# Decay rows in a buffer of their own, log decays made one head ahead, decayed queries in level two of a hybrid encoder layer

## The chip, the cores and the metric

The kernel runs on one core of a Trainium2 chip. The metric is the device time of one execution in microseconds. A core has five engines with instruction streams of their own: TensorE (PE, matrix products), VectorE (DVE), ScalarE (ACT), GpSimd (POOL) and SyncE (SP, which here only starts DMAs). They wait for each other through semaphores. The products read SBUF and write PSUM banks.

## The reference

One encoder layer over two sequences of 512 tokens, width 1024. One input projection feeds two groups of heads: neighbourhood attention (8 heads) and gated DeltaNet (4 heads of 128, both directions). The part that matters here, per DeltaNet head:

```
qkv = silu(dwconv_centred(concat(g_q, g_k, g_v)))      # 5 taps
q, k = l2norm(q) * dk**-0.5, l2norm(k)
gc = cumsum(g)                                         # log decays, per chunk
decay = exp(where(tril, gc_i - gc_j, -inf))
lower = where(strict, (k beta) k^T * decay, 0);  a = lower + I
solve a [u, w] = [v beta, k beta exp(gc)]
attn = q k^T * decay;  q_dec = q * exp(gc)
scan over chunks: v_new = u - w S;  o = q_dec S + attn v_new;  S = S cd + k_dec^T v_new
o = rmsnorm(o_forward + o_backward) * norm_w * silu(z)
```

The heads' outputs are concatenated with the attention's, projected, normalised, and followed by a gated MLP with a depthwise convolution of width 3 and a second norm.

## The kernel before, in words

The input is held transposed, split into a high and a low part; each projection is made of 24 products per sequence (8 slices of the width, 3 products each: high-high, low-high, high-low). Weights come in chunks of 512 KB: SP loads them into two raw buffers (L417), POOL splits each into high and low parts (L524, L527), and PE uses them in order. SP's loads wait for the split of an earlier chunk, POOL's splits for PE to have finished an older one, so all three follow one counter. Every engine's order of work is written out by hand, and an engine that waits holds up whatever is written behind the wait.

The program first does the attention pairs (`attend`, four pairs, with projections as filler on PE), then the four DeltaNet heads (`delta_head`, h = 0 to 3), the output projection, and the MLP.

One head, in the order in which its work depends on itself:

1. PE projects queries for sequence 0, multiplies keys by keys, and transposes the keys (L803, L808). ACT squares the transposed keys (`key_squares`, L1261); DVE makes the key scales from them (`key_scales`, L1643).
2. Two decay rows per head, broadcast to 128 partitions, come from DRAM into the buffer `egr` (`load_decays`, L465), which shares its place with `d_n`. DVE makes the log decays from them (`log_decays`, L1656) and ACT takes their exponential in place (L1296); the result `dt_` shares its place with `att`. ACT also takes the exponential of `egr` itself (L1301).
3. DVE convolves the queries of sequence 0, then makes the lower blocks (`lower`, L1668), joins and masks them (L1742, semaphore `masked`).
4. PE projects values for sequence 0 into bank 0 once the query convolution has read it, then folds the masked blocks (L820, semaphore `folded`), then projects values for sequence 1 and the gate. ACT centres the value projection (`centre`, L1245) and copies the folded blocks (L1306); SP stores them to DRAM and loads them back turned (L476 to L482).
5. DVE inverts the small blocks (`eliminate`, L1685 to L1700) and the inverses go through DRAM too. DVE expands them: first what PE needs for level 0 (x_1 and m_t, L1705), then, behind the decayed queries (`decayed_q`, L1679), what DVE itself updates (d_n, L1705).
6. Three levels (lv = 0, 1, 2) double the block size: PE makes two groups of products per sequence (L872, then L886 and L889), ACT copies between them, DVE updates and selects (L1785, L1786, L1724, L1728). PE puts pieces of the next head's key projection in between as filler; the last head has none.
7. A scan over four chunks (k = 0 to 3), then the sums for the norm (L942, L943). SP waits for those sums before it loads the next head's decay rows, since `d_n` is in use until then. The next head's keys are convolved, the norm is finished and the tile goes to `mix`.

`mix` has eight tiles: four from the attention pairs, four from the heads; all are read by the output projection (`high_mix` on ACT, `low_mix` on DVE).

Of the kernel before, what the change touches and what calls it, by code (L numbers as in the profile page):

```python
# [11 lines left out]
P = 128  # L12
# [35 lines left out]
FILL = 2  # L48
LN_EPS, RMS_EPS = 1e-5, 1e-6
# [36 lines left out]
def encoder_layer(nc, xT, x_tok, ln_row, w_gate, w_all, rpb, gdn_conv, gate_vec, a_log,  # L86
                  norm_w, ffn_conv, consts, nat_mask, y, block_dram, inverse_dram, x1_dram, decay_dram):
    from contextlib import ExitStack
    ctx = ExitStack()
    with ctx:  # L90
# [131 lines left out]
        dt_, egr = att, d_n  # L222
# [101 lines left out]
        mix_high, mix_ready = sem("mix_high"), sem("mix_ready")  # L324

# [55 lines left out]
        def unit(n):  # L381
            return n // BLOCKS, n % BLOCKS

# [28 lines left out]
        def _(sp):  # L412
# [54 lines left out]
            load_chunks(8, GDN0 + 4)  # L467
            sp.wait_ge(o_evac, 2 * PAIRS + 1)
            load_decays(0)
            load_chunks(GDN0 + 4, GDN0 + 6)  # L470

            def exchange(h, last_head):
# [27 lines left out]
                for n in range(8, 10):  # L500
                    load(raw(GDN0 + n), 4 * h + (GDN0 + n))
# [3 lines left out]
            load_chunks(GDN0 + 4 * GH + 6, CHUNKS)  # L505
# [11 lines left out]
        def _(pool):  # L517
# [29 lines left out]
            split_chunks(2, GDN0 + 4)  # L547
# [6 lines left out]
            def split_for_next(h, last_head):  # L554

                pool.wait_ge(inv_ready, h + 1)
# [4 lines left out]
                if not last_head:  # L561
                    split_later(h, 2)
                    split_later(h, 3)
# [38 lines left out]
        def _(pe):  # L602
# [189 lines left out]
            def delta_head(h, last_head):  # L792
# [21 lines left out]
                project(0, slot(GDN0 + 2), 0)  # L814
                pe.wait_ge(k_tok_ready, 2 * h + 1)
                for s in range(SEQS):
                    pe.wait_ge(masked, 2 * h + (s + 1))
                    for cc in range(CH):
                        n = s * CH + cc
                        ins = mm(ps[6][:, n * IB:(n + 1) * IB], tile(u_t[:, s, :], cc), fold, start=True, stop=True)  # L820
                ins.then_inc(folded, 1)
# [74 lines left out]
                for k in range(CH):  # L896
# [20 lines left out]
                    for g in range(GROUPS):  # L917
# [13 lines left out]
                        ins = mm(out, x_1[:, g, P:2 * P], tile(att[:, g, :], cc), start=k == 0 and g % 2 == 0,  # L931
# [189 lines left out]
        def _(act_e):  # L1121
# [84 lines left out]

            def attend(pair, last_pair):
# [6 lines left out]
                for n in range(1, UNITS + 2):  # L1214
                    if n >= 2:
                        turned(pair, n - 2)
                    if 2 <= n < UNITS:
                        exps(pair, n)
                    if not last_pair and n in done_at:
# [31 lines left out]
            def delta_head(h, last_head):  # L1251
# [64 lines left out]
                for lv in range(NL):  # L1316
                    for s in range(SEQS):
                        act_e.wait_ge(x1_done, 2 * NL * h + (2 * lv + s + 1))
                        nc.scalar.copy(x_1[:, s, :], ps[2 + s][:, :]).then_inc(x1_evac, 1)

                for k in range(CH):
# [9 lines left out]
                    if k < SEQS:  # L1331
                        if k == 0:

                            act_e.wait_ge(ud_ready, 4 * h + 4)
                            if last_head:
                                high_mix(0)
# [11 lines left out]
                nc.scalar.preload_act_table_set(LN_EXP)  # L1348
# [144 lines left out]
        def _(dve):  # L1493
# [90 lines left out]
            def attend(pair, last_pair):  # L1584
# [3 lines left out]
                for n in range(2, UNITS):  # L1588
                    biased(pair, n)
                    normalised(pair, n - 1)  # L1590
                    if n == 7:
# [13 lines left out]
            attend(PAIRS - 2, False)  # L1605
            attend(PAIRS - 1, True)


            def tile(ap, c):
                return ap[:, c * P:(c + 1) * P]  # L1610
# [28 lines left out]
            def delta_head(h, last_head):  # L1639
# [10 lines left out]
                def log_decays(g):  # L1650

                    s, d = g // 2, g % 2
                    dve.wait_ge(rows_landed, 32 * h + 32)
                    for cc in range(CH):
                        col = NEG_GC * 16 + d * 8 + s * CH + cc
# [420 lines left out]
```

## Time and profile before

| what | value |
|---|---|
| median of 3 runs | 1462.19 us (1462.02 to 1463.68) |
| the profiled execution | 1462.43 us, span 1460.6 us |
| granted PE clock, mean | 0.989 of full |
| busy: PE, DVE, ACT, POOL | 96%, 54%, 30%, 33% |
| granted PE clock, 241 to 636 us (the heads) | 0.96 |
| decay rows, SP issue to landing, 8 transfers of 512 KB | 4.8 us (median) |
| mean of a split's two halves, L524 and L527 | 1.895 and 2.539 us |
| POOL's wait for PE before the split at 176.35 us | 13.84 us |
| longest idle of DVE ahead of an update of the scan, L1820 | 2.1 us |
| idle of DVE ahead of the key convolution of head 2 | 2.59 us |
| idle of ACT ahead of the scan of head 1 | 3.74 us |
| a table load on ACT | 1.28 us |

The span is that of the instructions; the device time of the same execution is 1.8 us longer. A bracket at the end of a row gives how long the engine was idle ahead of it and who ended that. Rows of the chain are pieces that ended last, followed back from the end, so their times add up. Rows of a timeline may merge several instructions (x8), and successive instructions of DVE and ACT overlap by about a tenth of a microsecond.

### The profile page before, as it was taken

To read this page: it belongs to the slowest core of one execution; us is meant where nothing else is said; L and a number is where in the kernel's file an instruction comes from. 1 tells how busy PE (TensorE), PEld (TensorE's weight loads), DVE (VectorE), ACT (ScalarE), POOL (GpSimd) and SP (SyncE) were. 2 spreads that over 40 slices of the span, in tenths; PEclk is the share of its full clock that TensorE was granted. 3 is DMA by queue.
4 is the path that set the end of the run, shared out by engine and by line. 5 is a ranking of instruction groups with operands and counts; after the bars stand their busy time and mean duration, and the time that the engine had idled before them with its cause. 6 is when DMAs were issued, how large, how long until landed. Compare 5 with 4: busy or idle time off the path is not lost.

```text
span 1460.6 us, 18720 instructions
## 1 busy us (share of the span) xinstructions
PE 1397.9 (96%) x6959; PEld 1147.7 (79%) x6959; DVE 789.3 (54%) x1346; ACT 441.7 (30%) x924; POOL 479.7 (33%) x219
## 2 busy tenths in 40 slices
PE   7999998989899898799999999999999999999998
PEld 5777776778787787788878888888888888888886
DVE  4344446877958869742654344344344344225657
ACT  4233344427236164240532212211221222122220
POOL 3322221212121122116454334334334344454470
PEclk9999999999999999899999999999999999999999
DMA  8100111201102112032221111111111114111112
GB/s 248 45 30 30 34 40 44 50 9 59 41 15 64 29 59 49 15 130 86 102 87 44 56 45 43 57 43 43 57 43 43 57 43 187 57 43 46 55 57 101
DMA packets 49511, 87.15 MB, mean 60 GB/s; under 512 B 24432, under 2 KB 27184, under 8 KB 49456
## 3 DMA queue, kind: packets, MB, share of 16 engines
q1 hardware_dynamic: 44704, 70.41, 15.4%
q10 hardware_dynamic: 4752, 15.99, 2.8%
q8 instruction: 36, 0.59, 0.2%
q14 instruction: 19, 0.16, 0.0%
HBM read 76.66 MB, written 9.73 MB: 59 GB/s over the span
## 4 chain that ended last, share of the span: by engine, by line
issue 37%; PE 33%; DVE 15%; POOL 10%; DMA 2%; ACT 1%; POOLq 1%; SPq 0%; DVEq 0%; ACTq 0%
PE banks L639 11%; POOL w_hi L524 8%; PE banks L955 6%; PE banks L1055 3%; PE banks L614 2%; DVE qkv L1623 2%; PE banks L748 1%; DMA d_n<-decay_dram 1%; PE banks L773 1%; DVE m_t L1668 1%; DVE d_n L1786 1%; PE banks L761 1%; DVE inv L1697 1%; DVE outer L1694 1%; DVE att L1656 1%
## 5 line engine op out<-in xcount | busy, mean ns | idle before, releaser
L524 POOL TENSOR_TENSOR w_hi<-w_raw,one 128x1024 fp32r<-128x1024 f32 (+1 forms) x99 | 187.6, 1895 | 905.7 <-PE banks L614 376.0
L614 PE MATMUL banks<-x_hi,w_hi 128*128 128x512 f32 (+1 forms) x912 | 360.3, 395 | 19.1 <-POOL w_lo L527 8.9
L614 PE MATMUL banks<-x_hi,w_lo 128*128 128x512 f32 (+1 forms) x912 | 356.9, 391 | 0.0
L614 PE MATMUL banks<-x_lo,w_hi 128*128 128x512 f32 (+1 forms) x912 | 356.6, 391 | 0.0
L1907 DVE SCALAR_TENSOR_TENSOR cv<-banks,fw,cv 128x511 f32<-128x511 f32 x176 | 131.9, 750 | 261.7 <-ACT cv L1427 254.0
L527 POOL TENSOR_TENSOR w_lo<-w_raw,w_hi 128x1024 fp32r<-128x1024 f32 (+1 forms) x99 | 251.3, 2539 | 7.8
L614 PEld LDWEIGHTS banks<-x_hi,w_hi 128*128 128x128 f32 (+1 forms) x912 | 171.3, 188 | 58.5 <-issue 11.4
L614 PEld LDWEIGHTS banks<-x_hi,w_lo 128*128 128x128 f32 (+1 forms) x912 | 171.1, 188 | 37.5 <-issue 1.0
L614 PEld LDWEIGHTS banks<-x_lo,w_hi 128*128 128x128 f32 (+1 forms) x912 | 171.4, 188 | 36.9 <-issue 1.5
L1427 ACT ACTIVATE cv<-banks,fw_j 128x512 f32<-128x512 f32 x88 | 68.7, 780 | 336.9 <-PE banks L614 334.4
L1936 DVE TENSOR_TENSOR a_lo<-act,a_hi 128x1024 fp32r<-128x1024 f32 x39 | 65.5, 1684 | 96.1 <-ACT a_hi L1445 96.1
L1055 PE MATMUL banks<-w_hi,a_hi 128*128 128x512 f32 x288 | 112.0, 389 | 0.0
L1055 PE MATMUL banks<-w_hi,a_lo 128*128 128x512 f32 x288 | 112.0, 389 | 0.0
L1055 PE MATMUL banks<-w_lo,a_hi 128*128 128x512 f32 x288 | 112.0, 389 | 0.0
L639 PE MATMUL banks<-x_hi,w_hi 128*128 128x512 f32 x256 | 103.9, 406 | 0.0
L639 PE MATMUL banks<-x_lo,w_hi 128*128 128x512 f32 x256 | 103.3, 404 | 0.0
L639 PE MATMUL banks<-x_hi,w_lo 128*128 128x512 f32 x256 | 103.3, 404 | 0.0
L1445 ACT CAST a_hi<-act 128x1024 fp32r<-128x1024 f32 (+1 forms) x39 | 40.8, 1054 | 147.3 <-PE banks L1055 139.7
L1623 DVE SCALAR_TENSOR_TENSOR qkv<-banks,cw_all,qkv 128x510 f32<-128x510 f32 (+1 forms) x96 | 71.2, 749 | 12.1 <-ACT qkv L1245 8.8
L1917 DVE TENSOR_TENSOR act<-cv 128x512 f32 (+1 forms) x44 | 68.4, 1554 | 9.1 <-DVE cv L1907 8.9
L1564 DVE TENSOR_TENSOR s_sb<-banks,bm 128x512 f32<-128x512 f32 x32 | 22.1, 691 | 76.8 <-PE banks L748 76.8
L1055 PEld LDWEIGHTS banks<-w_lo,a_hi 128*128 128x128 f32 x288 | 54.1, 188 | 11.3
(206 smaller groups left out, 1999.9 us busy)
## 6 DMA issues: line engine op xcount, KB each, us to landing
w_raw<-w_all SPq DMA_DIRECT2D x102, 512.0 KB, 3.3
d_n<-decay_dram SPq DMA_DIRECT2D x8, 512.0 KB, 4.8
z_tok<-x_tok ACTq DMA_DIRECT2D x8, 512.0 KB, 5.6
x_dram<-z_tok ACTq DMA_DIRECT2D x8, 512.0 KB, 2.6
z<-x_dram ACTq DMA_DIRECT2D x8, 512.0 KB, 7.5
y<-z SPq DMA_DIRECT2D x7, 512.0 KB, 2.6
mix<-xT SPq DMA_DIRECT2D x12, 256.0 KB, 7.7
gb<-ln_row ACTq DMA_DIRECT2D x4, 512.0 KB, 7.9
```

The lines of the kernel that those rows point to most:

```text
L524: nc.gpsimd.tensor_tensor(w_hi[u][:, 0:n], w_raw[ru][:, 0:n], one[:, :].to_broadcast([P, n]), ALU.mult).then_inc(w_high, 1)
L527: nc.gpsimd.tensor_tensor(w_lo[u][:, 0:n], w_raw[ru][:, 0:n], w_hi[u][:, 0:n].bitcast(F32), ALU.subtract).then_inc(w_ready, 1)
L614: last = mm(ps[bank][0:cols, :], w[u][:, k * cols:(k + 1) * cols], seq(x[:, k, :], s), start=n == 0, stop=n == 3 * KT - 1)
L639: ins = mm(ps[s][:, :], w[u][:, k * P:(k + 1) * P], seq(x[:, k, :], s), start=i == 0, stop=i == 3 * KT - 1)
L955: ins = mm(ps[b][:, :], x[k][:, t * P:(t + 1) * P], w[u][:, cols], start=k == 0 and n == 0, stop=k == KT - 1 and n == 2)
L1055: ins = mm(ps[t][:, :], x[a][:, t * P:(t + 1) * P], w[u][:, cols], start=start and i == 0, stop=stop and i == 2)
L1427: A(cv[:, b, :], ps[b][:, :], ACT.Identity, scale=fw_j[:, x, 1:2], bias=fw_j[:, x, 3:4]).then_inc(up_center, 1)
L1445: nc.scalar.copy(a_hi[a][:, :], act[:, bass.ds(k, 1), :].rearrange("p a n -> p (a n)")).then_inc(a_high, 1)
L1623: ins = STT(dst[:, a:b], src[:, a + o:b + o], cw_all[:, 3 * h + x, tap:tap + 1], dst[:, a:b], ALU.mult, ALU.add)
L1907: ins = STT(cv[:, b, a:e], ps[b][:, a + o:e + o], fw[:, bass.ds(2 * j + x, 1), tap:tap + 1].rearrange("p a b -> p (a b)"), cv[:, b, a:e], ...
L1917: TT(act[:, bass.ds(j, 1), s * L:(s + 1) * L].rearrange("p a n -> p (a n)"), cv[:, s, :], cv[:, 2 + s, :], ALU.mult).then_inc(up_act, 1)
L1936: TT(a_lo[a][:, :], act[:, bass.ds(k, 1), :].rearrange("p a n -> p (a n)"), a_hi[a][:, :].bitcast(F32), ALU.subtract).then_inc(a_ready, 1)
```

## The change

- The decay rows get a place of their own, the first two tiles of `mix`. Their attention output is stored to DRAM (`mix_dram`) once two pairs are done, and ACT loads it back in the last head. `egr` therefore no longer shares with `d_n`.
- The log decays of head h have a buffer that alternates (`dt_(h)`: two further tiles of `mix`, or `att`). Those of head 0 are made during the attention; of a later head three of four groups are made in the scan of the head before, the fourth at the head's start. The rows of the next head are loaded once the decayed queries of this one are made.
- The decayed queries are made in the loop of levels at lv == 1, no longer between the expansions.
- The fold of the masked blocks stands inside the value projection, ahead of the slice FOLD_AT = 5 of 8.
- Weights: one chunk fewer is split ahead of the heads; a head's gate chunk is split once its blocks are masked. ACT centres the queries of sequence 1 ahead of the exponentials of `egr`, and loads its table ahead of the scan instead of behind it.

```diff
@@ places @@
+FOLD_AT = 5
-        dt_, egr = att, d_n
+        egr = mix[:, 0:2, :].rearrange("p k (s n) -> p (k s) n", s=SEQS)
+        decays = [mix[:, 6:8, :].rearrange("p k (s n) -> p (k s) n", s=SEQS), att[:, :, :]]
+        def dt_(h):
+            return decays[h % 2]
@@ SyncE @@
-            load_chunks(8, GDN0 + 4)
-            sp.wait_ge(o_evac, 2 * PAIRS + 1)
+            load_chunks(8, 12)
+            sp.wait_ge(o_evac, 2 * 2 + 1)
+            sp.dma_start(mix_dram, flat(mix[:, 0:2, :])).then_inc(mix_stored, 16)
+            sp.wait_ge(mix_stored, 16)
             load_decays(0)
-            load_chunks(GDN0 + 4, GDN0 + 6)
+            load_chunks(12, GDN0 + 5)
...
-                for n in range(6, 8):
+                for n in range(5, 7):
                     load(raw(GDN0 + n), 4 * h + (GDN0 + n))
                 if not last_head:
-
-                    sp.wait_ge(osum_done, 2 * h + 2)
+                    sp.wait_ge(qd_ready, 4 * h + 4)
                     load_decays(h + 1)
@@ GpSimd @@
-            split_chunks(2, GDN0 + 4)
+            split_chunks(2, GDN0 + 3)
...
+                pool.wait_ge(masked, 2 * h + 2)
+                split_later(h, -1)
                 pool.wait_ge(inv_ready, h + 1)
                 split_later(h, 0)
...
                 if not last_head:
                     split_later(h, 2)
-                    split_later(h, 3)
@@ TensorE @@
-                project(0, slot(GDN0 + 2), 0)
-                pe.wait_ge(k_tok_ready, 2 * h + 1)
-                for s in range(SEQS):
-                    pe.wait_ge(masked, 2 * h + (s + 1))
...
+                def fold_blocks(k):
+                    if k != FOLD_AT:
+                        return
+                    pe.wait_ge(k_tok_ready, 2 * h + 1)
+                    for s in range(SEQS):
+                        pe.wait_ge(masked, 2 * h + (s + 1))
+                        for cc in range(CH):
+                            n = s * CH + cc
+                            ins = mm(ps[6][:, n * IB:(n + 1) * IB], tile(u_t[:, s, :], cc), fold, start=True, stop=True)
+                    ins.then_inc(folded, 1)
+
+                project(0, slot(GDN0 + 2), 0, wait_k=fold_blocks)
@@ ScalarE @@
+            def decayed(h, g):
+                act_e.wait_ge(dt_ready, 4 * h + (g + 1))
+                A(dt_(h)[:, g, :], dt_(h)[:, g, :], ACT.Exp).then_inc(dt_exp, 1)
...
-                for g in range(GROUPS):
-                    act_e.wait_ge(dt_ready, 4 * h + (g + 1))
-                    A(dt_[:, g, :], dt_[:, g, :], ACT.Exp).then_inc(dt_exp, 1)
+                if h:
+                    decayed(h, GROUPS - 1)
...
                 key_norms()
+                centre(h, QX, 1)
                 for g in range(GROUPS):
                     A(egr[:, g, :], egr[:, g, :], ACT.Exp).then_inc(egr_ready, 1)
-                centre(h, QX, 1)
                 silu(QX, 0)
                 centre(h, VX, 0)
                 act_e.wait_ge(folded, h + 1)
...
+                    if last_head and lv == 1:
+                        act_e.wait_ge(qd_ready, 4 * h + 4)
+                        act_e.wait_ge(mix_stored, 16)
+                        act_e.dma_start(flat(mix[:, 0:2, :]), mix_dram).then_inc(mix_landed, 16)
+                nc.scalar.preload_act_table_set(LN_EXP)
...
+                    if not last_head and k == 2:
+                        decayed(h + 1, 0)
...
-                nc.scalar.preload_act_table_set(LN_EXP)
+                else:
+                    decayed(h + 1, 1)
+                    decayed(h + 1, 2)
@@ VectorE @@
-                for g in range(GROUPS):
-                    log_decays(g)
+                if h:
+                    log_decays(h, GROUPS - 1)
                 key_scales()
...
-                dve.wait_ge(silu_done, 6 * h + 4)
-                for g in range(GROUPS):
-                    decayed_q(g)
-
-                dve.wait_ge(qd_ready, 4 * h + 4)
...
+                    if lv == 1:
+                        dve.wait_ge(silu_done, 6 * h + 4)
+                        for g in range(GROUPS):
+                            decayed_q(g)
...
+                    if not last_head and k == 1:
+                        log_decays(h + 1, 0)
+                    if not last_head and k == 3:
+                        log_decays(h + 1, 1)
+                        log_decays(h + 1, 2)
```

ACT at the start of head 1, from the key squares to the copy of the folded blocks (`packed`); `att`, `d_n` and `mix` hold the decays, `qkv` the projections that are centred. Before:

```order
L1296 ACTIVATE att<-att 128x512 [waits dt_ready] x4
L1298 COPY k_tok<-banks 128x512 x2
L1268 ACTIVATE k_ln<-k_sq,eps 128x8 [waits k_squared]
L1270 ACTIVATE k_norm<-k_ln 128x8 [waits norm_ln]
L1301 ACTIVATE d_n<-d_n 128x512 x4
L1245 ACTIVATE qkv<-banks,cw_all 128x512 [waits proj_done]
L1254 ACT_TABLE_LOAD
L1254 ACTIVATE qkv<-qkv 128x512 [waits conv_done]
L1245 ACTIVATE qkv<-banks,cw_all 128x512 [waits proj_done]
L1306 COPY packed<-banks 128x128 [waits folded]
```

With the change:

```order
L1223 ACTIVATE att<-att 128x512 [waits dt_ready]
L1317 COPY k_tok<-banks 128x512 x2
L1288 ACTIVATE k_ln<-k_sq,eps 128x8 [waits k_squared]
L1290 ACTIVATE k_norm<-k_ln 128x8 [waits norm_ln]
L1265 ACTIVATE qkv<-banks,cw_all 128x512 [waits proj_done]
L1321 ACTIVATE mix<-mix 128x512 x4
L1274 ACT_TABLE_LOAD
L1274 ACTIVATE qkv<-qkv 128x512 [waits conv_done]
L1265 ACTIVATE qkv<-banks,cw_all 128x512 [waits proj_done]
L1325 COPY packed<-banks 128x128 [waits folded]
```

Three of the four exponentials of the decays are gone from here (they stand in the head before), and the centring behind `key_norms` (L1245, now L1265) comes ahead of the exponentials of the rows. In both, the centring that waits for the value projection stands ahead of the copy that waits for the fold.

PE around the fold of head 1 (`cst,u_t` are the fold matrix and the masked blocks; `x_hi,w_hi` and the like a projection). Before:

```order
L614 MATMUL banks<-x_hi,w_lo_69 128x512
L820 MATMUL banks<-cst,u_t 128x16 [waits masked,k_tok_ready]
L820 MATMUL banks<-cst,u_t 128x16 x3
L820 MATMUL banks<-cst,u_t 128x16 [waits masked]
L820 MATMUL banks<-cst,u_t 128x16 x3
L614 MATMUL banks<-x_hi,w_hi_68 128x512 [waits m_ready]
L614 MATMUL banks<-x_lo,w_hi_68 128x512
```

With the change:

```order
L622 MATMUL banks<-x_hi,w_lo_69 128x512
L831 MATMUL banks<-cst,u_t 128x16 [waits masked,k_tok_ready]
L831 MATMUL banks<-cst,u_t 128x16 x3
L831 MATMUL banks<-cst,u_t 128x16 [waits masked]
L831 MATMUL banks<-cst,u_t 128x16 x3
L622 MATMUL banks<-x_hi,w_hi_68 128x512
L622 MATMUL banks<-x_lo,w_hi_68 128x512
```

The fold comes nine products earlier in the order: before, the product behind it is the first of the next value projection (it waits for `m_ready`); now it is the 16th of the same one.

DVE in head 1, from the expansions to level 1 (`q_d` are the decayed queries, `d_n` the blocks that DVE updates). Before:

```order
L1705 TENSOR_TENSOR m_t<-packed,cst 128x512 x2
L1679 TENSOR_TENSOR q_d<-qkv,d_n 128x512 [waits egr_ready,silu_done]
L1679 TENSOR_TENSOR q_d<-qkv,d_n 128x512 [waits egr_ready] x3
L1705 TENSOR_TENSOR d_n<-packed,cst 128x512 [waits qd_ready]
L1705 TENSOR_TENSOR d_n<-packed,cst 128x512 x3
L1720 TENSOR_TENSOR u_t<-m_t,cst 128x512 [waits expanded]
L1720 TENSOR_TENSOR u_t<-m_t,cst 128x512
L1785 TENSOR_TENSOR d_n<-d_n,banks 128x512 [waits yy_done]
L1786 TENSOR_TENSOR d_n<-d_n,banks 128x512
L1724 TENSOR_TENSOR x_145<-d_n,cst 128x512 [waits w_updated]
```

With the change, at the place where they stood:

```order
L1736 TENSOR_TENSOR m_t<-packed,cst 128x512 x2
L1736 TENSOR_TENSOR d_n<-packed,cst 128x512 x4
L1751 TENSOR_TENSOR u_t<-m_t,cst 128x512 [waits expanded]
L1751 TENSOR_TENSOR u_t<-m_t,cst 128x512
L1815 TENSOR_TENSOR d_n<-d_n,banks 128x512 [waits yy_done]
L1816 TENSOR_TENSOR d_n<-d_n,banks 128x512
```

And at the place where they stand now, two updates later on DVE:

```order
L1755 TENSOR_TENSOR x_145<-d_n,cst 128x512 [waits w_updated]
L1759 TENSOR_TENSOR m_t<-d_n,cst 128x512 [waits v_updated]
L1751 TENSOR_TENSOR u_t<-m_t,cst 128x512 [waits x1_done] x2
L1710 TENSOR_TENSOR q_d<-qkv,mix 128x512 [waits egr_ready,silu_done]
L1710 TENSOR_TENSOR q_d<-qkv,mix 128x512 [waits egr_ready] x3
L1815 TENSOR_TENSOR d_n<-d_n,banks 128x512 [waits yy_done]
```

The four products of the decayed queries leave the place between `m_t` and `d_n`; behind `d_n` DVE goes straight to the first update, and makes the queries behind the blocks of the next level.

## Rows read from the trace of the kernel before

**Rows 1.** Chain that ended last, head 1: start us, us, what

```profile
350.95 4.29 DVE att L1656 x16
...
365.02 0.70 DVE u_t L1742
...
365.76 1.08 PE banks L820 x8
...
367.16 2.14 DMA block_dram<-packed
...
369.81 2.25 DMA blk<-block_dram
...
372.20 0.40 DVE blk L1685
```

**Rows 2.** DVE timeline, key scales of heads 0, 1, 2: start, us, engine, line, operation

```profile
258.03 0.17 DVE L1643 TENSOR_SCALAR k_inv<-k_sq 128x8 f32<-128x8 f32 x1 [5.16 <-ACT x L1261]
...
355.16 0.16 DVE L1643 TENSOR_SCALAR k_inv<-k_sq 128x8 f32<-128x8 f32 x1
...
451.71 0.16 DVE L1643 TENSOR_SCALAR k_inv<-k_sq 128x8 f32<-128x8 f32 x1
```

**Rows 3.** ACT timeline, first square of the keys in heads 0, 1, 2

```profile
255.82 0.28 ACT L1261 ACTIVATE x<-banks 128x128 f32<-128x128 f32 x1 [0.29 <-PE banks L808]
...
352.60 0.28 ACT L1261 ACTIVATE x<-banks 128x128 f32<-128x128 f32 x1 [0.29 <-PE banks L808]
...
448.25 0.28 ACT L1261 ACTIVATE x<-banks 128x128 f32<-128x128 f32 x1 [0.29 <-PE banks L808]
```

**Rows 4.** PE timeline, head 1, first value projection and the next one

```profile
359.07 0.47 PE L614 MATMUL banks<-x_hi,w_hi 128*128 128x512 f32 x1 [0.67 <-DVE qkv L1623]
...
362.59 0.39 PE L614 MATMUL banks<-x_hi,w_hi 128*128 128x512 f32 x1
...
366.68 0.49 PE L614 MATMUL banks<-x_hi,w_hi 128*128 128x512 f32 x1
...
368.62 0.40 PE L614 MATMUL banks<-x_hi,w_lo 128*128 128x512 f32 x1
```

**Rows 5.** ACT timeline, head 1, centring and the copy of folded blocks

```profile
364.83 0.69 ACT L1245 ACTIVATE qkv<-banks,cw_all 128x512 f32<-128x512 f32 x1 [1.98 <-PE banks L614]
366.87 0.27 ACT L1306 COPY packed<-banks 128x128 f32<-128x128 f32 x1 [1.34 <-PE banks L820]
```

**Rows 6.** DVE timeline, head 1, levels 0 and 1

```profile
391.38 2.49 DVE L1679 TENSOR_TENSOR q_d<-qkv,d_n 128x512 f32<-128x512 f32 x4
...
397.65 0.68 DVE L1785 TENSOR_TENSOR d_n<-d_n,banks 128x512 f32<-128x512 f32 x1
...
402.45 1.29 DVE L1720 TENSOR_TENSOR u_t<-m_t,cst 128x512 f32<-128x512 f32 x2
406.19 0.69 DVE L1785 TENSOR_TENSOR d_n<-d_n,banks 128x512 f32<-128x512 f32 x1 [2.45 <-PE banks L889]
```

**Rows 7.** PE timeline, level 0 of heads 0 and 1

```profile
292.74 2.02 PE L872 MATMUL banks<-x,u_t 128*128 128x128 f32 x16 [2.35 <-issue]
...
389.76 3.59 PE L872 MATMUL banks<-x,u_t 128*128 128x128 f32 x16 [2.34 <-issue]
...
395.29 1.06 PE L889 MATMUL banks<-m_t,x 128*128 128x128 f32 x8
```

**Rows 8.** Stretches: from:to, us, then busy us of each engine, granted PE clock

```profile
245.80:249.80 4.00, 4.00 (x10) 3.13 (x11) 3.89 (x9) 1.15 (x2) 0.00 (x0) 0.50 0.46 176
358.00:366.70 8.70, 7.86 (x43) 6.36 (x41) 8.56 (x24) 5.48 (x10) 4.30 (x2) 1.00 0.19 60
389.70:393.10 3.40, 3.34 (x17) 3.37 (x17) 3.40 (x6) 0.58 (x1) 0.00 (x0) 0.54 0.00 0
```

**Rows 9.** Chain that ended last, second group of level 1, heads 0 and 1

```profile
305.06 2.05 PE banks L872 x8
...
402.08 1.13 PE banks L872 x8
```

More of the change, by code:

```diff
@@ L324, in encoder_layer @@
         mix_high, mix_ready = sem("mix_high"), sem("mix_ready")
+        mix_stored, mix_landed = sem("mix_stored"), sem("mix_landed")
         out_step, out_done, out_evac, gb_landed = (
@@ L493, in exchange @@
                                      rows[:, i0:i0 + INST // 2, :]).then_inc(landed, 16)
-                for n in range(6, 8):
+                for n in range(5, 7):
                     load(raw(GDN0 + n), 4 * h + (GDN0 + n))
                 if not last_head:
-                    sp.wait_ge(osum_done, 2 * h + 2)
+                    sp.wait_ge(qd_ready, 4 * h + 4)
                     load_decays(h + 1)
-                for n in range(8, 10):
+                for n in range(7, 9):
                     load(raw(GDN0 + n), 4 * h + (GDN0 + n))
@@ L504, in _ @@
                 exchange(h, h == GH - 1)
-            load_chunks(GDN0 + 4 * GH + 6, CHUNKS)
+            load_chunks(GDN0 + 4 * GH + 5, CHUNKS)
             for t in range(TILES):
@@ L813, in delta_head @@
                 pe.wait_ge(conv_done, 6 * h + 3)
-                project(0, slot(GDN0 + 2), 0)
-                pe.wait_ge(k_tok_ready, 2 * h + 1)
-                for s in range(SEQS):
-                    pe.wait_ge(masked, 2 * h + (s + 1))
[L818 to L821, printed above, removed]
+                def fold_blocks(k):
[9 more added lines that the diff above has]
+                project(0, slot(GDN0 + 2), 0, wait_k=fold_blocks)
                 pe.wait_ge(m_ready, 4 * h + 4)
@@ L928, in delta_head @@
                             pe.wait_ge(qd_ready, 4 * h + 4)
-                        ins = mm(out, x_1[:, g, P:2 * P], tile(att[:, g, :], cc), start=k == 0 and g % 2 == 0,
+                        ins = mm(out, x_1[:, g, P:2 * P], tile(dt_(h)[:, g, :], cc), start=k == 0 and g % 2 == 0,
                                  stop=k == CH - 1 and g % 2 == 1)
@@ L1218, in attend @@
                         exps(pair, n)
+                    if last_pair and 2 <= n < 2 + GROUPS:
+                        decayed(0, n - 2)
                     if not last_pair and n in done_at:
@@ L1335, in delta_head @@
                             if last_head:
+                                act_e.wait_ge(mix_landed, 16)
                                 high_mix(0)
@@ L1582, in attended, with tile, log_decays, attend @@
                     ps[6 + s][:, :].rearrange("p (b r c) -> p r b c", b=BLOCKS, r=ROWS)).then_inc(o_evac, 1)
-            def attend(pair, last_pair):
+            def tile(ap, c):
+                return ap[:, c * P:(c + 1) * P]
+            def log_decays(h, g):
+                s, d = g // 2, g % 2
+                dve.wait_ge(rows_landed, 32 * h + 32)
+                for cc in range(CH):
+                    col = NEG_GC * 16 + d * 8 + s * CH + cc
+                    ins = STT(tile(dt_(h)[:, g, :], cc), tile(egr[:, g, :], cc), sc[:, h, col:col + 1], negm[d],
+                              ALU.add, ALU.add)
+                ins.then_inc(dt_ready, 1)
+            def attend(pair, last_pair, decays_from=UNITS):
                 biased(pair, 0)
@@ L1590, in attend @@
                     normalised(pair, n - 1)
+                    if n >= decays_from:
+                        log_decays(0, n - decays_from)
                     if n == 7:
@@ L1604, in _ @@
             step.leave(PAIRS // 2 - 1)
[L1605 removed]
+            attend(PAIRS - 2, False, UNITS - GROUPS)
             attend(PAIRS - 1, True)
[L1609 to L1610 removed]
             dve.wait_ge(par_landed, 48)
@@ L1648, in key_scales @@
                     dve.wait_ge(scales_ready, h + 1)
[L1650 to L1655, printed above, removed]
-                        ins = STT(tile(dt_[:, g, :], cc), tile(egr[:, g, :], cc), sc[:, h, col:col + 1], negm[d],
-                                  ALU.add, ALU.add)
-                    ins.then_inc(dt_ready, 1)
                 def lower(g):
@@ L1996, in build @@
     decay_dram = nc.dram_tensor("decay_dram", (2, GH, T), F32, kind="Internal").ap()
+    mix_dram = nc.dram_tensor("mix_dram", (P, 2 * T), F32, kind="Internal").ap()
     encoder_layer(nc, y=y, block_dram=block_dram, inverse_dram=inverse_dram, x1_dram=x1_dram, decay_dram=decay_dram,
-                  **args)
+                  mix_dram=mix_dram, **args)
 def shape_constants():
```

6 lines of the change are left out of this document (3 added, 3 removed).

## The prediction, made before the changed kernel was run

> **What bounds the kernel now.** I read the busy shares, then the chain of waits over the four DeltaNet heads (241 to 634 us), then the timelines of TensorE (PE), VectorE (DVE) and ScalarE (ACT) around the places that the change touches. PE is busy nearly all the time, and outside the heads its products follow each other almost without a gap; there only transfers and splits could hurt. Inside a head the chain is a round trip between engines, so what counts is who comes last.
>
> In head 1 that chain runs so [rows 1]: 16 log-decay steps on DVE end at 355.24, then key scales, query convolution, the lower blocks and two masks, the last of which ends at 365.72; PE folds the blocks, ACT copies them, two DMAs turn them (store from 367.16, load from 369.81), and DVE starts the elimination at 372.20. From there DVE is last as far as the levels, where PE and DVE alternate. Head 1 stands for heads 1 to 3; head 0 enters differently.
>
> **Log decays in the head before.** They leave the path, but the next instruction, the key scales, also needs ACT's squares of the keys. Head 0 shows it: its decays are made early, and DVE then sits idle 5.16 us until the squares are done [rows 2]. There the key scales start 2.21 us after ACT's first square (258.03 less 255.82) [rows 2, 3]. Squares need the transposed keys, which PE makes behind the query projection; nothing of that moves. So in head 1 the key scales could start at 352.60 + 2.21 = 354.81 instead of 355.16: 0.35 us gained, not 4.29. In head 2, where the rows' transfer was slower, 448.25 + 2.21 = 450.46 against 451.71: 1.25 us. Head 3 is as head 1. Sum: -1.95 us. Below this it could give 0, if the one group of decays that is left at the head's start were late; it has some 4 us of idle DVE for four steps of 0.27 us (4.29 / 16).
>
> The moved decays cost nothing where they land. Four steps (1.07 us) stand in the scan where DVE idles up to 2.1 us, eight (2.14 us) ahead of the key convolution, where it idles 2.59 us; ACT's table load (1.28 us) moves to where ACT idles 3.74 us; its two exponentials (about 0.56 us each) take the load's old place. If such a cover failed, the excess would be paid once a head, some tenths.
>
> **The fold inside the value projection.** Here something is lost. Before, the 24 products of the first value projection are done when the last mask comes. Now the wait for both masks stands ahead of the 16th product. In head 1 the 16th started at 362.59, 3.52 us after the first [rows 4], and the masks end at about 365.4 (365.72 less 0.35): PE stops about 3 us with nine products in hand. The fold comes no earlier, since DVE sets it. But the projection ends later, and on ACT the centring of that very projection stands ahead of the copy of the folded blocks. Nine products behind the fold last from 366.68 to 368.62 + 0.40 = 2.34 us [rows 4]; ACT takes them up 0.04 us later and its centring holds the copy back by another 0.6 of its 0.69 us [rows 5]. The copy then starts at 366.68 + 2.34 + 0.04 + 0.60 = 369.66 instead of 366.87: 2.8 us later, and with it store, load and elimination. Before, DVE had 0.1 us left there (372.06, when the load lands, against 372.20) [rows 1], so 2.7 us a head, in all four heads: +10.8 us. From below: even with the copy in time, the value convolution (about 3.1 us) and two short fills would end near 373.2 and cost 1.0 us a head (+4.0).
>
> From above: in that stop PE does little for about 4 us (wait, fold, wait, fold), and its clock can fall. The row of 358.00 to 366.70, with a shorter such stretch, still shows 1.00; that of 245.80, behind PE's long wait at the start of head 0, 0.50, with 10 products in 4.00 us [rows 8]. At that pace nine products take 9 x (0.40 - 0.24) = 1.5 us more. Between 0 and 1.5 us a head I take half: +3.0 us.
> The Trainium skill (TensorE: Matmul & The Clock Gate, Part 1) says that the clock depends on how busy the array has lately been, and that being throttled is its idle state, so it speaks against adding a stop. By it the upper end would hold in each head, +6.0 instead of +3.0. The trace agrees only in part: after 2.34 us of waiting the products ran at half pace, after 2.35 us at full pace [rows 7].
>
> **Decayed queries in level one.** (The change's loop calls it lv == 1, the second of three levels.) The four products of 2.49 us leave the place between two expansions, where they were on the path [rows 6], so DVE reaches the first update of level 0 2.45 us earlier. Then PE may be late: its products of level 0 for the first sequence end at 395.29 + 1.06 = 396.35, 6.6 us after it began at 389.76, while DVE took them up at 397.65 [rows 6, 7]. Only 1.3 us were spare, so 1.3 us are gained where PE's first 16 products take 3.59 us, and all 2.45 where they take 2.02, as in head 0 [rows 7]. The slow case is the half clock (0.54 over that stretch) [rows 8]. I take 1.9 us for heads 0 to 2 and 2.4 us for head 3, which has no filler products: -8.1 us; bounds -5.2 and -9.8.
>
> In the new place DVE waited 2.45 us for PE [rows 6], just as long as the products take: no more than 0.1 us is paid, unless that level runs faster than in head 1. A second gain: in three heads (0, 2, 3) level 1 ran at half clock, since PE stood idle between the levels; its second group took 2.05 us in head 0 against 1.13 in head 1 [rows 9]. With DVE earlier that idle time shrinks to what head 1 has: 0.9 x 3 = -2.7 us; bounds 0 and -2.7.
>
> **Queues.** SyncE now stores two tiles (1 MB) and waits for that, then loads the decay rows, all ahead of the 12th chunk of weights. GpSimd still waited 13.8 us for PE at the split in question, so several us of delay are covered; were they not, PE would wait for weights once. The split of the gate chunk moves behind the masks; it takes 1.9 + 2.5 us, and 33 products of 0.24 us (7.9 us) lie between the fold and its user. The tiles come back during the last head's levels over ACT's queue, over 10 us before they are read. All at 0.
>
> **Sum.** -1.95 + 10.8 + 3.0 - 8.1 - 2.7 = +1.05 us. The profiled execution has 1462.43 us (span 1460.6 and 1.8 around it), 0.24 above the median of the runs. Forecast: 1462.43 + 1.05 = 1463.5 us, less 0.24: about 1463.3. A measurement of this kernel can tell about 0.2% (2.9 us) from no change; the forecast lies inside.
>
> **Rivals.**
> - Faster: the clock holds in the stop, and level 0 runs at full pace. -1.95 + 10.8 - 9.8 - 2.7 = -3.65: about 1458.6. For it: the row with 1.00 around the old fold. Against it: the stop is twice as long as there. If moreover the copy were not late (only 1.0 a head), -10.4: 1452; the order of ACT speaks against that. Should the decays give all their 4.29 us in three heads, some 11 us more would go; the 5.16 us of head 0 say no. Together 0.31.
> - Slower, one mechanism: the stop in the value projection lowers PE's clock in every head. +10.8 + 6.0 for the late copy, only -5.2 from the queries as level 0 stays at half pace, no gain in level 1, -1.95: +9.65, about 1472. It decides as soon as the nine products take clearly over 3 us in most heads. For it: 0.50 after the longer wait. Against it: 2.35 us passed unpunished [rows 7]. From +2.9 us up: 0.29.
> - The forecast, within 2.9 us of before: 0.40. Two sizeable terms of opposite sign nearly cancel.
>
> So faster 0.31, same 0.40, slower 0.29. The range takes in both clock cases and nearly the whole way to the cheap fold: 1453 to 1472; the forecast's own part is 1459.3 to 1465.1.
>
> **What would show it.** Right, step by step: DVE idle some 4 us ahead of the key scales in all heads; PE waiting for a mask ahead of the fold with nine products behind it; the copy of the blocks starting over 9 x 0.24 us after the fold; DVE waiting for a DMA ahead of the elimination by 1.5 to 3 us; no query products ahead of the expansions, and a first update of level 0 that waits for PE or comes at once. Wrong: an elimination that starts no later after the masks than the 6.5 us of before (372.20 less 365.72), which would make the kernel about 0.7% faster; or PE waiting for weights in the attention part; or log decays that hold up the scan.

## The result and the profile after

| | before | with the change |
|---|---|---|
| median of 5 runs | 1462.19 us (1462.02 to 1464.63) | 1473.77 us (1468.45 to 1475.6) |
| ratio, 95% interval | | 1.0073 (1.0055 to 1.0090) |
| profiled execution, span | 1462.43, 1460.6 us | 1473.57, 1471.8 us |

The changed kernel is slower by 0.73%: the slower rival, which had a chance of 0.29, and 1.8 us above the top of the range. The page of the changed kernel, busy time and the chain by engine:

```profile
PE 1408.7 (96%) x6959; PEld 1156.7 (79%) x6959; DVE 790.2 (54%) x1346; ACT 441.3 (30%) x924; POOL 479.4 (33%) x219
...
PE 39%; issue 37%; POOL 10%; DVE 10%; ACT 2%; DMA 1%; POOLq 1%; SPq 0%; DVEq 0%; ACTq 0%
```

PE has 10.8 us more busy time than before (1397.9) for the same products: they ran slower. The heads tell where. The table cuts each head at six events of the timelines: the start of ACT's first square of the keys, the end of DVE's last mask, the start of the elimination, of the first update and of the scan's first mask on DVE, and the end of PE's last sum over `d_n`. It adds up four heads of the profiled execution (us); e1 and so on are the experiments below.

| stretch | before | after | e1 | e2 | e3 | e4 | e5 | e8 | e11 |
|---|---|---|---|---|---|---|---|---|---|
| first key square to last mask | 53.1 | 51.1 | 51.1 | 51.1 | 51.1 | 51.1 | 51.1 | 39.1 | 39.0 |
| last mask to elimination | 26.4 | 46.0 | 26.7 | 36.4 | 39.8 | 31.9 | 26.8 | 30.6 | 29.2 |
| elimination to first update | 101.8 | 95.5 | 94.0 | 91.6 | 95.0 | 93.0 | 101.2 | 91.7 | 91.6 |
| first update to scan | 70.9 | 67.8 | 68.0 | 66.8 | 68.2 | 68.2 | 67.6 | 68.0 | 66.4 |
| scan to the sums' end | 100.0 | 101.2 | 101.3 | 101.0 | 100.0 | 101.0 | 101.3 | 100.0 | 97.1 |

Before against after, in hundredths: -2.05 + 19.62 - 6.28 - 3.13 + 1.26 = 9.4 us when the output projection starts (9.5 by its own rows), and 1.7 us more behind it: the 11.2 us of the spans. One row carries the loss.

Head 1, the chain (start, us, what), against [rows 1]:

```profile
355.48 2.18 ACT x L1281 x16
...
367.56 0.70 DVE u_t L1773
368.31 1.06 PE banks L831 x8
369.37 14.67 PE banks L622 x57
...
393.58 2.49 issue
396.07 2.53 PE banks L885 x16
```

The log decays have gone from its head. Behind the fold it no longer goes over the copy and the two DMAs: it stays on PE, with the nine products that the fold's wait held up and the 48 of the next two projections. But PE is not the bound as far as level 0: it stands 2.49 us ("issue") ahead of that level, and starts when the first of DVE's expansions (`x<-packed,cst`, below) is done. DVE's late start is in the next rows.

PE of the changed kernel, head 1 (timeline), against [rows 4, 7]:

```profile
364.87 0.39 PE L622 MATMUL banks<-x_hi,w_lo 128*128 128x512 f32 x1
367.07 1.04 PE L831 MATMUL banks<-cst,u_t 128*128 128x16 f32 x8 [1.81 <-DVE u_t L1773]
368.31 1.06 PE L831 MATMUL banks<-cst,u_t 128*128 128x16 f32 x8 [0.20 <-DVE u_t L1773]
369.22 0.47 PE L622 MATMUL banks<-x_hi,w_hi 128*128 128x512 f32 x1
...
370.33 0.63 PE L622 MATMUL banks<-x_lo,w_hi 128*128 128x512 f32 x1
...
372.04 0.63 PE L622 MATMUL banks<-x_hi,w_lo 128*128 128x512 f32 x1
...
396.07 2.53 PE L885 MATMUL banks<-x,u_t 128*128 128x128 f32 x16 [2.49 <-issue]
```

ACT, against [rows 5]:

```profile
372.70 0.69 ACT L1265 ACTIVATE qkv<-banks,cw_all 128x512 f32<-128x512 f32 x1 [6.67 <-PE banks L622]
373.29 0.26 ACT L1325 COPY packed<-banks 128x128 f32<-128x128 f32 x1
```

And DVE, against [rows 2, 6]:

```profile
357.69 0.17 DVE L1684 TENSOR_SCALAR k_inv<-k_sq 128x8 f32<-128x8 f32 x1 [4.16 <-ACT x L1281]
...
378.52 0.39 DVE L1716 COPY blk<-packed 64x256 f32<-64x256 f32 x1 [1.56 <-DMA blk<-block_dram]
...
395.28 1.29 DVE L1736 TENSOR_TENSOR x<-packed,cst 128x512 f32<-128x512 f32 x2
...
402.66 0.69 DVE L1815 TENSOR_TENSOR d_n<-d_n,banks 128x512 f32<-128x512 f32 x1 [1.15 <-PE banks L902]
...
408.67 2.49 DVE L1710 TENSOR_TENSOR q_d<-qkv,mix 128x512 f32<-128x512 f32 x4
```

Read together: PE stops 1.81 us ahead of the fold; of the nine products behind it the fifth to ninth take 0.63 us instead of 0.39; ACT sits idle 6.67 us until they are done, centres, and only then copies the blocks that were folded at 369.37. DVE waits for their DMA. The granted clock from the fold to the copy, heads 0 to 3 (from:to, us, busy PE, PEld, DVE, ACT, POOL, then clock), against [rows 8]:

```profile
267.40:275.30 7.90, 7.84 (x29) 6.91 (x30) 4.12 (x6) 0.51 (x1) 4.26 (x2) 0.57 0.00 0
...
367.00:373.20 6.20, 5.93 (x27) 5.05 (x28) 4.13 (x6) 0.50 (x1) 4.26 (x2) 0.75 0.00 0
464.80:472.60 7.80, 7.62 (x27) 6.54 (x28) 4.13 (x6) 0.54 (x1) 4.26 (x2) 0.56 0.01 2
564.10:571.90 7.80, 7.74 (x28) 6.78 (x29) 4.12 (x6) 0.54 (x1) 4.26 (x2) 0.56 0.01 2
```

In three heads almost the whole stretch, fold included, ran at the lower level (1.2 GHz); in head 1 about half of it.

### The profile page after: what moved, and what is told of

Its sections match the earlier page's. It is cut to its first block, busy times and chain, and to the rows that moved or that the text cites. A ratio compares the mean times of both kernels' runs of the same rounds, so it can differ in the third digit from the quotient of the medians.

```text
span 1471.8 us, 18722 instructions
## 1 busy us (share of the span) xinstructions
PE 1408.7 (96%) x6959; PEld 1156.7 (79%) x6959; DVE 790.2 (54%) x1346; ACT 441.3 (30%) x924; POOL 479.4 (33%) x219
## 4 chain that ended last, share of the span: by engine, by line
PE 39%; issue 37%; POOL 10%; DVE 10%; ACT 2%; DMA 1%; POOLq 1%; SPq 0%; DVEq 0%; ACTq 0%
PE banks L647 12%; POOL w_hi L531 8%; PE banks L622 6%; PE banks L968 5%; PE banks L1068 3%; PE banks L885 1%; PE banks L756 1%; DVE qkv L1664 1%; PE banks L781 1%; DVE m_t L1699 1%; DVE d_n L1816 1%; PE banks L769 1%; PE banks L936 1%; PE banks L944 1%; PE banks L927 1%
## 5 line engine op out<-in xcount | busy, mean ns | idle before, releaser
L622 PE MATMUL banks<-x_hi,w_hi 128*128 128x512 f32 (+1 forms) x912 | 364.0, 399 | 17.5 <-POOL w_lo L534 8.3
L622 PE MATMUL banks<-x_lo,w_hi 128*128 128x512 f32 (+1 forms) x912 | 360.3, 395 | 0.0
L1068 PEld LDWEIGHTS banks<-w_hi,a_hi 128*128 128x128 f32 x288 | 54.1, 188 | 11.3
```

Source lines behind the costliest of these rows:

```text
L622: last = mm(ps[bank][0:cols, :], w[u][:, k * cols:(k + 1) * cols], seq(x[:, k, :], s), start=n == 0, stop=n == 3 * KT - 1)
L1068: ins = mm(ps[t][:, :], x[a][:, t * P:(t + 1) * P], w[u][:, cols], start=start and i == 0, stop=stop and i == 2)
```

## The experiments

Theory A: the stop inside the value projection, with products in hand and ACT's order behind them, makes the whole loss; the other parts gain. Rivals stand with each run. Each ratio is to the kernel before on the same chip; it took 1462.16 us beside e1 to e4, 1463.55 beside e5 to e8 and 1463.88 beside e9 to e11, so times of different groups differ by up to 1.7 us for that alone.

**e1, the fold back behind the projection.**

```diff
-                project(0, slot(GDN0 + 2), 0, wait_k=fold_blocks)
+                project(0, slot(GDN0 + 2), 0)
+                fold_blocks(FOLD_AT)
```

> The changed kernel with the fold back behind the first value projection; all else as changed. Theory A (the stop inside the value projection and the slow products behind it hold back ACT's centring, and with it the copy of the folded blocks; together 19.6 us over four heads, from the last mask to the elimination 10.3, 10.3, 11.8 and 11.8 us instead of 6.5 to 6.9): the stretch from last mask to elimination is 6.5 to 6.9 us again in all heads, time 1451 to 1455 us. Theory B (the elimination is late because of another part: ACT's new order, SyncE's queue, the mask itself): the stretch stays above 9 us, time about 1474 us.

Measured 1452.43 us, ratio 0.9936 (0.9920 to 0.9952). Last mask to elimination 6.50, 6.49, 7.18 and 6.49 us (in the changed kernel it is 12.07, 10.27, 11.78 and 11.83 us; the expectation's 10.3 for head 0 is wrong). ACT's copy follows the fold again, and level 0 starts at full pace here behind as long a wait as before:

```profile
362.98 0.27 ACT L1326 COPY packed<-banks 128x128 f32<-128x128 f32 x1 [1.35 <-PE banks L831]
```

```profile
385.86 2.02 PE L886 MATMUL banks<-x,u_t 128*128 128x128 f32 x16 [2.38 <-issue]
```

So one line of the change turns 0.6% gained into 0.7% lost. Theory B is out.

**e2, ACT's copy ahead of the centring.**

```diff
-                centre(h, VX, 0)
                 act_e.wait_ge(folded, h + 1)
                 nc.scalar.copy(packed..., ps[6]...).then_inc(fold_copied, 1)
+                centre(h, VX, 0)
```

> The changed kernel with ACT's copy of the folded blocks ahead of its centring of the value projection; the fold stays ahead of the sixth slice. Theory A: the copy starts within 0.1 us of the fold's end, but DVE still takes the value convolution ahead of the elimination and that waits for the nine late products: the elimination comes only 1.0 to 1.5 us earlier a head, time 1468 to 1470 us. Rival C (ACT's order alone makes the loss): masks to elimination back to 6.5 us, time about 1454 us.

Measured 1459.94 us, ratio 0.9982 (0.9973 to 0.9991): between the two. The order on ACT is not all (rival C), since now the value convolution ends last, as expected:

```profile
364.41 0.27 ACT L1324 COPY packed<-banks 128x128 f32<-128x128 f32 x1 [3.37 <-PE banks L831]
...
368.87 3.10 DVE L1664 SCALAR_TENSOR_TENSOR qkv<-banks,cw_all,qkv 128x510 f32<-128x510 f32 x4 [2.61 <-ACT qkv L1265]
...
372.44 0.38 DVE L1716 COPY blk<-packed 64x256 f32<-64x256 f32 x1
```

But the size was missed by 8 us: the elimination came 2.4 us earlier a head, the fold ran at full pace in all heads here (2.3 us against 3.1 to 3.4 in three heads of the changed kernel), and level 0 too (elimination to first update 91.6). PE's order was not touched, and it stopped as long ahead of the fold (1.77 to 1.81 us); its clock fell later, so the same stop cost 5.9 us of slow products over four heads here.

**e3, PE kept busy in the stop.**

```diff
                     pe.wait_ge(k_tok_ready, 2 * h + 1)
+                    for j in range(8):
+                        mm(ps[6][:, :], w_hi[slot(GDN0 + 2)][:, 0:P], seq(x_hi[:, 0, :], 0), start=True, stop=True)
                     for s in range(SEQS):
```

> The changed kernel with eight extra full-width products on PE ahead of the fold's wait (about 1.9 us; the fold overwrites what they write). Theory A with the clock as its second half: PE stays at full pace, the nine products behind the fold take 2.2 to 2.4 us instead of 3.3 to 4.1, the copy comes 2.7 us late a head as the prediction's order term has it, time 1464 to 1466 us. Rival D (the clock falls with the narrow products of the fold whatever stands ahead of it, or it was only the order): no faster than the changed kernel, 1473 to 1476 us.

Measured 1467.22 us, ratio 1.0033 (1.0021 to 1.0045), 1.2 us above the expected range. With the extra products the clock held in heads 0 and 2; in 1 and 3 it fell behind the fold:

```profile
267.50:273.00 5.50, 5.24 (x31) 4.55 (x31) 4.35 (x8) 0.84 (x3) 3.99 (x2) 1.00 0.00 0
364.10:371.00 6.90, 6.63 (x31) 5.48 (x30) 4.25 (x7) 0.71 (x2) 4.26 (x2) 0.75 0.00 0
462.30:468.00 5.70, 5.44 (x32) 4.72 (x32) 4.53 (x7) 1.06 (x3) 4.22 (x2) 1.00 0.01 3
558.80:565.70 6.90, 6.64 (x30) 5.58 (x30) 4.21 (x7) 0.68 (x2) 4.26 (x2) 0.75 0.00 0
```

This separates the loss in two. Where the clock held, the copy comes 3.88 and 3.91 us behind the last mask, against 1.16 before: 2.73 us a head is the price of the order. In the changed kernel it comes 6.74, 5.04, 6.60 and 6.60 us behind; the clock is the rest, 24.98 - 4 x 3.89 = 9.4 us. Rival D is out as a whole, but not for heads 1 and 3: PE did not stand still ahead of the fold there and only 0.27 us within it, against 0.2 in the kernel before, and the products behind it still ran slow. That the clock's share comes from the stop alone is not shown.

**e4, FOLD_AT = 7 instead of 5.**

> The changed kernel with the fold ahead of the eighth slice of the value projection instead of the sixth: three products behind it instead of nine. Theory A: the copy is late by 3 x 0.24 to 3 x 0.43 us and 0.6 us of centring, 1.3 to 1.9 us a head, instead of 3.8 to 5.6; time 1458 to 1461 us. Theory B: no change, 1474 us.

Measured 1456.30 us, ratio 0.9967 (0.9955 to 0.9980), 1.7 us below the expected range. The stop is short (0.41 to 0.46 us), and from the fold to the copy the clock holds in heads 0 and 1, and nearly in head 3; here heads 1 and 2:

```profile
363.53 1.04 PE L831 MATMUL banks<-cst,u_t 128*128 128x16 f32 x8 [0.46 <-DVE u_t L1773]
```

```profile
363.50:367.30 3.80, 3.57 (x23) 3.24 (x24) 3.66 (x6) 0.64 (x2) 2.43 (x2) 1.00 0.00 0
457.50:462.00 4.50, 4.21 (x22) 3.67 (x23) 4.14 (x6) 0.71 (x2) 3.08 (x2) 0.76 0.02 4
```

The copy is 1.4 us late in three heads and 1.9 in one. The loss falls with the products behind the fold, as theory A has it; the stop is shorter too, and this run does not part the two.

**e5, on e1: the decayed queries back between the expansions** (`decayed_q` out of the loop of levels, to where it stood; it still reads its own decay buffer).

> The kernel of e1 (fold behind the projection) with the decayed queries back between the two expansions, from their own decay buffer. Theory A (the move takes 2.49 us of DVE out of the path and so brings PE into levels 0 and 1 at a faster clock; elimination to first update 94.0 instead of 101.8 us over four heads, first update to scan 68.0 instead of 70.9): both go back to the sums of before, time 1452.4 + 7.7 + 2.9 = 1463 us. Rival F (only the first of the two comes from the queries, the faster level 1 from something else in the change): 1460 us.

Measured 1460.79 us, ratio 0.9984 (0.9969 to 0.9998), 8.4 us above e1 (7.0 by the two ratios), and the table has the reason: elimination to first update 101.2 instead of 94.0 us, but first update to scan 67.6, as fast as with the move. Rival F holds: the queries earn the first term, and the faster levels do not need them. Second group of level 1 of head 0 in e5:

```profile
306.25 1.13 PE L886 MATMUL banks<-x,u_t 128*128 128x128 f32 x8 [1.27 <-DVE x L1756]
```

In the kernel before the same products took 2.05 us [rows 9], also behind a wait of 1.27 us. The waits of that level are the same with the queries on the path (1.88 and 1.27 us against 2.01 and 1.27); only the pace differs, so the 2.9 us are once more the clock. What kept it up there with the change is not shown.

**e6, on e1: all log decays at the head's start; e10, on e6: their rows loaded late as well.**

```diff
                 if h:
-                    log_decays(h, GROUPS - 1)
+                    for g in range(GROUPS):
+                        log_decays(h, g)
```

(The exponentials on ACT likewise, and their calls in the scan go; e10 also waits for `osum_done` instead of `qd_ready` ahead of `load_decays`.)

> The kernel of e1 with all four groups of log decays and their exponentials at the head's start again (heads 1 to 3), from the separate buffer; their rows are still loaded early. Theory A (the key scales wait for ACT's squares in any case, so the move earns only the 2.0 us by which first square to last mask is shorter): since the rows now lie ready, DVE has its decays done long before the squares, and the time stays within 0.5 us of e1 or rises by up to 2, 1452 to 1454.5 us. Rival G (the move takes 3.2 us off the path in each of three heads): 1462 us.

> The kernel of e6 (all log decays at the head's start) with the next head's decay rows loaded only once the sums of this head are done, as in the kernel before. Theory A (what the log-decay part earns comes from loading the rows early into a place of their own, not from where the decays are made): first square to last mask goes back from 12.77 us to 13.1, 14.0 and 13.1 us in heads 1 to 3, 2.0 us in all. Rival K (place of the decays matters, or the rows come in time anyway): 12.8 us in all heads.

Measured: e6 1452.95 us, ratio 0.9939 (0.9918 to 0.9961), as e1; first square to last mask 12.77 us in each head. e10 1457.94 us in one run; that stretch is 12.93, 15.17 and 13.63 us in heads 1 to 3, so 3.4 us are lost, more than the 2.0 expected. Decays and key scales of head 2 in e6, then key scales of head 2 and decays of head 3 in e10:

```profile
439.20 4.29 DVE L1620 SCALAR_TENSOR_TENSOR mix<-mix,sc,cst 128x128 f32<-128x128 f32 x16
444.50 0.17 DVE L1681 TENSOR_SCALAR k_inv<-k_sq 128x8 f32<-128x8 f32 x1 [1.01 <-ACT x L1282]
```

```profile
446.67 0.16 DVE L1681 TENSOR_SCALAR k_inv<-k_sq 128x8 f32<-128x8 f32 x1
...
538.99 4.29 DVE L1620 SCALAR_TENSOR_TENSOR att<-mix,sc,cst 128x128 f32<-128x128 f32 x16 [2.01 <-DMA mix<-decay_dram]
```

With the rows there early, DVE has all 16 steps done and still waits 1.01 us for ACT. What earns is the place of the rows' own, which lets them be loaded early; making the decays in the head before earns nothing.

**e7, on e1: the query convolution ahead of the key scales; e8, the changed kernel (FOLD_AT = 5) with that and with the copy of e2.**

```diff
-                key_scales()
                 convolve(h, QX, 0)
+                key_scales()
```

> The kernel of e1 with the query convolution of sequence 0 (3.1 us) ahead of the key scales on DVE, in the 4.2 to 5.2 us in which DVE waits for ACT's squares. Theory A (that idle time is what the moved log decays opened and nothing used): masks end 3.0 us earlier a head; but the fold now waits for the whole value projection, which starts only 0.3 to 0.7 us earlier, so the gain is 1.0 to 1.5 us a head, time 1446 to 1449 us. Rival H (the squares or key scales are held up by it, or PE sets the pace there): 1452 us or above.

> The changed kernel (fold ahead of the sixth slice) with the query convolution ahead of the key scales and ACT's copy ahead of its centring. Theory A: the masks end about when PE reaches the fold, so it stops for under 1 us and the nine products behind the fold stay at full pace; the copy follows the fold at once. Last mask to elimination is about 7 us as the value convolution ends last, and the masks are 3 us earlier: 2.3 us a head better than e1, time 1441 to 1446 us. Rival I (the fold in mid projection costs the clock whatever the stop): 1450 us or above.

Measured: e7 1450.00 us, ratio 0.9904 (0.9882 to 0.9927); e8 1442.75 us, 0.9855 (0.9831 to 0.9880). In e7 masks end 3.0 us sooner, and the fold gives 1.7 to 2.0 us of it back, since it waits for the whole projection; the expected time was missed by 1 us, with level 0 slow in three heads. In e8 the same fold inside the projection that lost 19.6 us costs PE nothing, as the masks come by the time PE gets there (DVE, then PE of head 1):

```profile
348.23 3.10 DVE L1664 SCALAR_TENSOR_TENSOR qkv<-banks,cw_all,qkv 128x510 f32<-128x510 f32 x4 [0.39 <-ACT qkv L1265]
351.99 0.17 DVE L1684 TENSOR_SCALAR k_inv<-k_sq 128x8 f32<-128x8 f32 x1 [0.67 <-ACT x L1281]
```

```profile
358.60 0.40 PE L622 MATMUL banks<-x_hi,w_lo 128*128 128x512 f32 x1
358.84 1.85 PE L831 MATMUL banks<-cst,u_t 128*128 128x16 f32 x16
360.54 0.48 PE L622 MATMUL banks<-x_hi,w_hi 128*128 128x512 f32 x1
```

No wait ahead of the fold, and the clock was 1.00 over 358 to 366 us. Last mask to elimination is still 7.65 us a head against 6.5: the value convolution ends last, which is the lower case of the prediction (1.0 us a head).

**e9, on e1: the low part of the first output tile (`low_mix(0)`, last head) behind the scan's last chunk (k == CH - 1) instead of its first. e11, on e8: that, and the two fills of `inv` ahead of the value convolution.**

> The kernel of e1 with the low part of the first output tile (last head only, on DVE) at the end of the scan instead of behind its first chunk, where it took 3.13 us beside GpSimd's split (1.70 us in the kernel before) and PE then waited and fell to half clock. Theory A: that is where the last head's scan got 1.3 us longer (26.27 us from its first mask to the sums, 25.0 in the other heads); without it the stretch falls below 25 us, to 22 to 23.5. Rival J (the extra time in the last head is PE's own, the low part was covered): 25 to 26.3 us.

> The kernel of e8 with two further moves on DVE: the two fills of the inverse ahead of the value convolution, in the 1.1 us that DVE waits there, and the low part of the first output tile at the end of the scan. Theory A: 0.4 us a head from the fills and 1.3 to 3 us from the last head's scan: 1438 to 1441 us. Rival (the elimination waits for its blocks, or the scan's clock decides): 1442 to 1443 us.

Measured: e9 1447.12 us in one run, the last head's scan to the sums 22.14 us instead of 26.27. e11 1437.64 us, ratio 0.9823 (0.9810 to 0.9836), the fastest of all and 0.4 us below the expected range; last mask to elimination 7.29 us a head (e8: 7.65), the scan 22.14.

## Why the prediction was wrong, point by point

- **Log decays**: right in size (-1.95 forecast, -2.05 measured; 0.34, 1.25 and 0.33 us in heads 1 to 3) and in the reason, that the squares come last. That the gain needs the early rows alone (e6, e10) was not seen. Nor was it seen that the 4 us of idle DVE which the change opens ahead of the key scales was worth more than the decays: a 3.1 us convolution fits there (e8).
- **The order on ACT and PE**: right. The copy was forecast 2.8 us late a head; it was 2.73 late where the clock held (e3).
- **The clock in the stop**: the step that failed. It was put at "nine products take 9 x (0.40 - 0.24) = 1.5 us more", of which half was taken, +3.0 us; it measured 9.4. Two things were missing. The clock fell in every head, not in half of them; and it was already down during the fold, whose 16 narrow products then took 3.1 to 3.4 us instead of 2.3 in three heads. The nine products lost 6.6 us in all, the fold 2.7. Per product, half pace costs 0.43 - 0.23 = 0.20 us, from start to start, more than the 0.16 of the prediction: its row of ten products in 4.00 us [rows 8] counts a tenth that began 0.02 us before the stretch ended. The stop itself was 1.8 us, not 3, since the first half of the fold waits for the first mask alone. When in it the clock falls, none of these rows tells: e2, with the same stop, lost 5.9 us. The sentence on the Trainium skill (TensorE: Matmul & The Clock Gate, Part 1) pointed the right way, and its upper end, +6.0, would have forecast 1466; its weight against one row with 1.00 [rows 8] was misjudged. The granted clock of the changed kernel agrees with it in all four heads (0.56 to 0.75 from the fold to the copy).
- **Decayed queries**: -8.1 forecast, -6.3 measured. Heads 0 to 2 gave 1.3 us each, the end for a slow level 0, head 3 gave 2.4. The full 2.5 us a head is there when PE holds its clock, as in e2 and e8.
- **Level 1**: -2.7 forecast, -3.1 measured, but the cause given, the queries, is refuted by e5.
- **Queues**: those named cost nothing. Not foreseen were 1.3 us in the last head and 1.7 us behind the output projection, both below.
- The sum misses by 10.1 us: the elimination 19.6 instead of 13.8 (+5.8; at the copy it is 10.9 for the order and 9.4 for the clock, of which 0.7 is lost again in DVE's spare time ahead of the elimination), the queries +1.8, last head and MLP +2.9, the rest -0.5. The slower rival had the mechanism and its place, and put it at 1472. That it came so near is in part luck: it has no gain in level 1 (-3.1 measured), too little for the clock (+6.0 against 9.4) and nothing for the last head and the MLP (+2.9), and these errors offset each other.

## What to carry over

An instruction put inside a run of products must not have to wait there: look up when its input is ready against when the engine arrives, and what is queued behind it on the engine that reads the run's end. A gap that a change opens on an engine earns nothing until something that is on the path is put into it. And price a stop of PE with the slow pace of all that follows it until the pace is back, the narrow products included.

## What the runs showed of the hardware

The pace after a stop is not a fixed price. Behind a wait of 1.93 us at the start of the MLP the changed kernel ran at 0.64 and the one before at 1.00 (each time PE's first product behind the wait, then the stretch: from:to, us, ..., clock, DMA share, GB/s):

```profile
754.77 0.50 PE L622 MATMUL banks<-x_hi,w_hi 128*128 128x512 f32 x1 [1.93 <-DVE x_lo L1918]
...
754.70:759.50 4.80, 4.73 (x14) 3.77 (x15) 1.51 (x3) 0.97 (x2) 0.00 (x0) 0.64 0.33 114
```

```profile
745.23 0.50 PE L614 MATMUL banks<-x_hi,w_hi 128*128 128x512 f32 x1 [1.93 <-DVE x_lo L1883]
...
745.20:750.00 4.80, 4.77 (x21) 3.92 (x22) 1.50 (x2) 0.98 (x2) 0.00 (x0) 1.00 0.36 113
```

That is 14 products against 21 and most of the 1.7 us. What decides it was not settled. In eight of the twelve kernels with the change (this one and e1 to e11) the clock fell there, in four it did not.

DVE's subtraction of two SBUF tiles waits for GpSimd's. In the last head (timeline of the changed kernel):

```profile
622.45 2.35 POOL L534 TENSOR_TENSOR w_lo<-w_raw,w_hi 128x1024 fp32r<-128x1024 f32 x1
622.75 3.13 DVE L1678 TENSOR_TENSOR m_lo<-mix,m_hi 128x1024 fp32r<-128x1024 f32 x1
626.19 2.08 PE L927 MATMUL banks<-x,u_t 128*128 128x128 f32 x8 [2.57 <-DVE x L1837]
```

It ends at 625.88, 1.08 us behind GpSimd's end at 624.80; alone it takes 1.22 us (e9, below). It took 1.70 us before, where it began 0.62 us ahead of GpSimd's end, and ended again 1.08 us behind it:

```profile
614.18 2.35 POOL L527 TENSOR_TENSOR w_lo<-w_raw,w_hi 128x1024 fp32r<-128x1024 f32 x1
615.91 1.70 DVE L1637 TENSOR_TENSOR m_lo<-mix,m_hi 128x1024 fp32r<-128x1024 f32 x1
```

It is so throughout: in the changed kernel 27 subtractions of this shape began while an instruction of GpSimd ran, took 1.73 to 3.41 us and ended 1.08 to 1.09 us behind it; the other 25 took 1.21 to 1.23 us. In the last head PE waits 2.57 us for the instruction behind the subtraction (L1837) and comes back at half pace. In e9 it stands where nothing waits, and the same products take 1.20 us:

```profile
602.69 1.20 PE L928 MATMUL banks<-x,u_t 128*128 128x128 f32 x8
...
613.11 1.22 DVE L1679 TENSOR_TENSOR m_lo<-mix,m_hi 128x1024 fp32r<-128x1024 f32 x1
```

The Trainium skill (SBUF — State Buffer, "SBUF: two separate sides") says that the two engines share a pair of ports as an exclusive lock for a whole instruction; these durations agree with it.
